# Decoder trunk: each MLP's first weight quarters requested during the projection before it, and attention scores from split queries and keys in a new order

## Time and profile before

| | us |
|---|---|
| median of 3 runs | 1056.5 (1055.74 to 1056.93) |
| the profiled execution's own time | 1058.89 |
| its span | 1057.1 |
| PE busy | 1035.2 (98%) |
| DVE busy | 813.7 (77%) |
| ACT busy | 644.7 (61%) |
| granted clock, mean | 0.994 |

### The profile page before, as it was taken

One profiled execution on the slowest core, in us unless ns is written; L12 is line 12 of the kernel. 1 busy time (PEld: TensorE's weight loads), 2 busy tenths in 40 slices (PEclk: granted clock), 3 DMA queues, 4 the chain that ended last, 5 costly groups with the idle time before them and its releaser, 6 DMA issues.

```text
span 1057.1 us, 15296 instructions
## 1 busy us (share of the span) xinstructions
PE 1035.2 (98%) x5920; PEld 885.5 (84%) x5920; DVE 813.7 (77%) x1157; ACT 644.7 (61%) x940; POOL 108.2 (10%) x133
## 2 busy tenths in 40 slices
PE   8999999999999999999999999999899999999995
PEld 6777889979989989988877777779888988988984
DVE  6988875886896896898656666566598698698697
ACT  7698864745745745665336656566664664664665
POOL 1000021121111101100000000012011011011012
PEclk9999999999999999999999999999999999999998
DMA  7222288498498498462321111167779678779672
GB/s 253 91 81 80 81 229 211 117 252 231 115 256 228 118 258 230 115 173 88 112 63 58 60 60 41 60 187 145 207 143 246 209 151 244 203 152 252 193 156 104
DMA packets 47592, 165.29 MB, mean 156 GB/s; under 512 B 5408, under 2 KB 5536, under 8 KB 47392
## 3 DMA queue, kind: packets, MB, share of 16 engines
q1 hardware_dynamic: 31536, 109.59, 30.2%
q0 software_dynamic: 15552, 53.48, 27.7%
q10 hardware_dynamic: 432, 1.24, 0.3%
HBM read 159.05 MB, written 2.10 MB: 152 GB/s over the span
## 4 chain that ended last, share of the span: by engine, by line
PE 87%; DVE 5%; DMA 5%; ACT 1%; issue 1%; SPq 0%; DVEq 0%; ACTq 0%
PE ps L1982 27%; PE ps L2017 27%; PE ps L1849 21%; DMA w_raw<-weights 5%; PE ps L2080 4%; PE ps L2139 2%; PE ps L2165 2%; DVE w_lo L1120 1%; PE ps L1908 1%; PE ps L2154 1%; DVE value L1499 1%; ACT w_hi L618 1%; DVE acc L1149 0%; DVE q L1452 0%; DVE x_lo L1401 0%
## 5 line engine op out<-in xcount | busy, mean ns | idle before, releaser
L1982 PE MATMUL ps<-x_hi,w_hi 128*128 128x256 f32 x896 | 255.2, 285 | 3.3 <-DVE cols L1170 2.0
L1982 PE MATMUL ps<-x_lo,w_hi 128*128 128x256 f32 x896 | 254.4, 284 | 0.0
L1982 PE MATMUL ps<-x_hi,w_lo 128*128 128x256 f32 x896 | 254.3, 284 | 0.0
L618 ACT ACTIVATE w_hi<-w_raw 128x1024 fp32r<-128x1024 f32 x134 | 140.5, 1055 | 170.2 <-DMA w_raw<-weights 127.8
L1120 DVE TENSOR_TENSOR w_lo<-w_raw,w_hi 128x1024 fp32r<-128x1024 f32 x134 | 163.9, 1224 | 89.4 <-ACT w_hi L618 88.9
L1120 DVE TENSOR_TENSOR w_lo<-q,w_hi 128x1024 fp32r<-128x1024 f32 x144 | 176.3, 1227 | 42.9 <-ACT w_hi L618 42.0
L618 ACT ACTIVATE w_hi<-q 128x1024 fp32r<-128x1024 f32 x144 | 150.9, 1052 | 93.4 <-PE ps L1982 42.1
L2017 PE MATMUL ps<-w_hi,a_hi 128*128 128x512 f32 x448 | 176.2, 393 | 1.8 <-DVE w_lo L1120 1.2
L1982 PEld LDWEIGHTS ps<-x_hi,w_hi 128*128 128x128 f32 x896 | 172.9, 193 | 4.1 <-DVE cols L1170 2.2
L2017 PE MATMUL ps<-w_hi,a_lo 128*128 128x512 f32 x448 | 174.6, 390 | 0.0
L2017 PE MATMUL ps<-w_lo,a_hi 128*128 128x512 f32 x448 | 174.5, 390 | 0.0
(11 more groups left out here) (218 smaller groups left out, 1666.8 us busy)
## 6 DMA issues: line engine op xcount, KB each, us to landing
w_raw<-weights SPq DMA_DIRECT2D x134, 512.0 KB, 4.4
q<-weights POOLq DMA_DIRECT2D x96, 512.0 KB, 8.1
q<-weights SPq DMA_DIRECT2D x64, 512.0 KB, 4.6
x<-x_t SPq DMA_DIRECT2D x8, 256.0 KB, 6.6
y_t<-value SPq DMA_DIRECT2D x8, 256.0 KB, 2.3
acc<-work POOLq DMA_DIRECT2D x6, 256.0 KB, 3.3
rstd<-work POOLq DMA_DIRECT2D x6, 256.0 KB, 3.5
w_raw<-weights SPq DMA_DIRECT2D x4, 256.0 KB, 4.7
```

The lines of the kernel that those rows point to most:

```text
L618: nc.scalar.activation(w_hi[:, t % RING, :], src, ACT.Copy).then_inc(whi_done, 1)
L1982: ins = nc.tensor.matmul(to, w[:, t % RING, ws], o[:, op, j, :], start=fresh and j == 0 and f % 2 == 0 and n == 0, stop=j == PAIRS - 1 and ...
```

## The change

Two parts.

1. Loads. `q1` and `q2` now lie at the start of their memory region, over `in_hi` (first layer) and `h_hi` (second). SP requests A21 for `q2` and `q1` in the middle of the projection's own loads (`first_quarters`), after waiting for `tile_done` of the products that used that place. POOL's `add_first` now also issues the A11 addition to `q1`, ahead of `accumulate`.
2. Scores. Queries and keys are split: ACT copies each to fp32r (`query_hi`, `key_hi`), DVE subtracts in place (`query_lo`, `key_lo`), and a score is three fp32r matmuls for each map in place of one float32 matmul. The lists of PE, ACT and DVE in the attention are in a new order; `scores(h, 0)` and `scores(h, 1)` are neighbours, for the last head also 2 and 3.

```diff
         region = ExitStack()
+        q1 = sb("q1", [P, 2, TILE], F32, region)
+        q2 = sb("q2", [P, 2, TILE], F32, region)
...
+        kq_lo = sb("kq_lo", [P, 2, 2, S], F32R, early)
+        early.close()
         kq = sb("kq", [P, 2, 2, S], F32)
...
+        kq_hi = (att_hi[:, HEADS - 2:, :], att_lo[:, HEADS - 2:, :])
...
-                    elif layer:
-                        sp.wait_ge(scores_mm, QB * HEADS)
                     else:
-                        sp.wait_ge(olo_done, O_M0)
+                        sp.wait_ge(tile_done, (T_OUT, T_O)[layer])
...
             for r in range(RAWS, R_MLP0):
                 load_ring(r, r)
+                if r == R_MLP0 - RING:
+                    first_quarters(0)
...
+                if r == R_MLP1 - RAWS - 1:
+                    first_quarters(1)
...
             def add_first(layer, g):
                 add_quarter(layer, g, "q2", A22, loaded=0)
+                add_quarter(layer, g, "q1", A11, loaded=0)
...
+            def key_hi(h):
+                act.wait_ge(bank_read, T_QK - SHIFT + 2 * h + 2)
+                nc.scalar.activation(kq_hi[0][:, h % 2, :], kq[:, h % 2, 0, :], ACT.Copy).then_inc(kq_hi_done, 1)
...
+            def key_lo(h):
+                dve.wait_ge(kq_hi_done, 2 * h + 2)
+                nc.vector.tensor_tensor(kq_lo[:, h % 2, 0, :], kq[:, h % 2, 0, :], kq_hi[0][:, h % 2, :],
+                                        ALU.subtract).then_inc(kq_lo_done, 1)
...
-                    pe.wait_ge(bank_read, T_QK - SHIFT + 2 * h + 2)
+                    pe.wait_ge(kq_lo_done, 2 * h + 2)
...
+                for i, (q, k) in enumerate(((q_hi, k_hi), (q_lo, k_hi), (q_hi, k_lo))):
+                    for c in range(2):
+                        rows = slice(c * HEAD_DIM, (c + 1) * HEAD_DIM)
+                        ins = nc.tensor.matmul(ps[:, BANK_SCORES + 2 * (j % 2) + c, 0:n], q[rows, :], k[rows, :],
+                                               start=i == 0, stop=i == 2)
...
             for h in range(HEADS - 1):
                 kq_part(h + 1, 0)
+                kq_part(h + 1, 1)
+                if h > 1:
+                    back(h - 2)
+                kq_part(h + 1, 2)
+                if h:
+                    attend(h - 1, 0)
+                    transposes(h - 1, 2)
+                    attend(h - 1, 1)
                 scores(h, 0)
...
                 scores(h, 1)
...
                 if h:
                     transposes(h - 1, 3)
...
+                kq_part(h + 1, 4)
+                kq_part(h + 1, 5)
+                kq_part(h + 1, 6)
                 transposes(h, 0)
...
+                kq_part(h + 1, 7)
+                scores(h, 2)
                 transposes(h, 1)
...
                 scores(h, 3)
```

More of the change, by code:

```diff
@@ L341, in build @@
         sub_gain_done = sem("sub_gain_done")
+        kq_hi_done = sem("kq_hi_done")
+        kq_lo_done = sem("kq_lo_done")
         scores_mm = sem("scores_mm")
@@ L1010, in _ @@
             act.wait_ge(sub_gain_done, 1)
-            split_hi(T_QK + RING)
-            for h in range(HEADS):
-                last = h == HEADS - 1
+            query_hi(0)
+            key_hi(0)
+            for h in range(HEADS - 2):
+                split_hi(T_QK + 2 * h + RING)
                 if h:
                     transposed(h - 1, 2)
-                split_hi(T_QK + 2 * h + 1 + RING if not last else T_QK + 2 * h + RING)
+                split_hi(T_QK + 2 * h + 1 + RING)
+                if h:
+                    transposed(h - 1, 3)
@@ new lines, in _ @@
+            h = HEADS - 2
+            split_hi(T_QK + 2 * h + RING)
+            transposed(h - 1, 2)
+            split_hi(T_QK + 2 * h + 1 + RING)
+            transposed(h - 1, 3)
+            exps(h, 0)
+            squares(h - 1)
+            exps(h, 1)
+            sub_guess_of(h - 1)
+            transposed(h, 0)
+            split_hi(T_O + 2)
+            scaled(h - 1)
+            transposed(h, 1)
+            query_hi(h + 1)
+            key_hi(h + 1)
+            attended_hi(h - 1)
@@ L1051, in _ @@
+            split_hi(T_O + 3)
+            transposed(h + 1, 2)
+            transposed(h + 1, 3)
+            squares(h + 1)
+            sub_guess_of(h + 1)
+            scaled(h + 1)
+            attended_hi(h + 1)
             residual_step(1, T_O, T_O - SHIFT, N_M1, ("mlp_norm", NCH))
@@ L1745, in _ @@
             key(0)
[L1746 to L1751, removed]
-            for h in range(HEADS - 2):
+            query_lo(0)
+            key_lo(0)
+            for h in range(HEADS - 2):
+                biased(h, 0)
+                biased(h, 1)
+                split_lo(T_QK + 2 * h + RING)
+                combined(h, 0)
+                if h:
+                    variance(h - 1)
@@ L1753, in _ @@
                 query(h + 1)
+                combined(h, 1)
+                if h:
+                    sub_newton(h - 1)
                 split_lo(T_QK + 2 * h + 1 + RING)
+                biased(h, 2)
+                key(h + 1)
+                query_lo(h + 1)
                 biased(h, 3)
                 combined(h, 2)
-                key(h + 1)
                 if h:
                     attended_lo(h - 1)
-                split_lo(T_QK + 2 * h + 2 + RING)
+                key_lo(h + 1)
@@ L1761, in _ @@
+                combined(h, 3)
                 halved(h)
[L1762 to L1769, removed]
-            h = HEADS - 2
[L1771 to L1776, removed]
@@ L1788, in _ @@
             biased(h, 3)
+            query_lo(h + 1)
+            key_lo(h + 1)
+            attended_lo(h - 1)
             combined(h, 2)
-            split_lo(T_QK + 2 * h + 1 + RING)
-            attended_lo(h - 1)
+            halved(h)
             combined(h, 3)
+            biased(h + 1, 0)
+            biased(h + 1, 1)
+            combined(h + 1, 0)
+            split_lo(T_O + 2)
             variance(h)
             sub_newton(h)
+            combined(h + 1, 1)
+            biased(h + 1, 2)
@@ L1795, in _ @@
+            biased(h + 1, 3)
+            combined(h + 1, 2)
             attended_lo(h)
+            combined(h + 1, 3)
+            split_lo(T_O + 3)
+            variance(h + 1)
+            sub_newton(h + 1)
+            attended_lo(h + 1)
             residual_step(1, T_O)
```

125 lines of the change are left out of this document (58 added, 67 removed).

## The result

The changed kernel takes 1042.68 us (median of 4 runs, 1042.32 to 1043.27), against 1056.55 for the kernel before on the same chip (4 runs): ratio 0.987, 95% interval 0.9853 to 0.9887. I had forecast 1041.0 with a range of 1036 to 1047.5; the time lies inside, 1.7 us over the forecast. The profiled execution took 1043.27 us, 15.6 less than the one before. That is the predicted 15.5 to 0.1; between the medians it is 13.9, since the profiled execution before lay 2.3 over its median and this one 0.6. The closeness of 15.6 to 15.5 is partly luck: the three stages that I forecast gained 14.5, two of the three terms are off in opposite directions, and about 1 us comes from start-up work that the change does not touch.

What follows compares the result with a forecast made beforehand. PE, busy 98% of the span, was taken as the bound. Part 1 (loads) 10.2 us plus part 2 (scores) 5.3 made 15.5 off the 1056.5 median: 1041.0 us, range 1036 to 1047.5.

Steps and rivals of the forecast that it cites:

- First MLP, 3.6 predicted: Moved loads and additions end PE's 2.2 us pause before up product 3 and the 1.2 GHz stretch behind it.
- (b): Rival: A12 tile still late in the first MLP or both MLPs, 1044 to 1047 us; chance 0.11 with (e).
- the clock's term: First MLP: the 3.41 us stretch at 1.2 GHz goes with the pause, worth 1.4 us.
- Second MLP, 6.6 predicted: DVE on time 1.5 us, pause before the transposes 3.4, slow stretch about 1.7, all gained from moved loads.
- no longer shares the engines with the quarter loads and additions: Second MLP: ACT's tile comes clear of them, so DVE enters the last residual step on time: 1.5 us.
- the 1.7 us for the slow stretch: Second MLP: stretch holds 13 matmuls where 31 would fit, less 0.7 us of pause already counted: about 1.7 us.
- Attention, 5.3 predicted: Part 2 on PE: 0.66 us for each of six middle heads (4.0), first head 0.3, last 1.0.
- A visit: Attention: entering the score blocks costs 0.30 us; four visits a head become three, in the last head two.
- (a): Rival in the scores: the two maps do not run together in fp32r, part 2 loses about 6, 1052 us; chance 0.07.
- (c): Rival in the attention: key_lo late by a steady 1 us a head, part 2 gives nothing, 1046 to 1047; chance 0.08.
- (d): Rival in the attention: key_lo chain over 3.1 us late a head, change slower, 1063 us at 4 us; chance 0.04.
- (e): Rival in the loads: first_quarters waits so late for tile_done that nothing moves; chance 0.11 together with (b).

Runs made afterwards that it cites:

- e6: Changed kernel with POOL's A11 additions to q1 back behind the squares, loads still early: 1045.15 us, ratio 0.9884.
- e4: Changed kernel with the second MLP's first quarters requested one ring load earlier: 1041.9 us, ratio 0.9849.
- e1: Kernel before with the loads' edits only, float32 scores and old orders kept: 1048.2 us, ratio 0.9911.
- e3: Changed kernel with float32 score products, no splits of queries and keys, new orders and loads kept: 1045.55 us, ratio 0.9884.
- e9: Changed kernel with transposes(h - 1, 3) again between scores(h, 0) and scores(h, 1) in six heads: 1045.64 us, ratio 0.9887.
- e8: Changed kernel with map 1's score matmuls left out: 1041.51 us (one run).
- e5: Changed kernel with each score block's fp32r matmuls reordered, three of map 0 and then three of map 1: 1044.04 us, ratio 0.9869.
- e11: Changed kernel measured again with no edit: 1044.55 us, ratio 0.9885.
- e2: Kernel before with the scores' edits only, loads and additions of the first quarters as before: 1048.55 us, ratio 0.9914.

## Why the prediction was right, and where it was not

**First MLP, 3.6 predicted, 3.8 measured.** Pause and slow stretch gone. I expected the tile in 6 to 7 us, with a limit of 8.5; it took 4.5. Rival (b) says that the load's own length is not in the trace before. It is: the ring load of 696.21 landed in 3.5 us. e6 shows that the additions' place does it. It also shows that the lower clock did not follow from the pause by need: e6 has the pause without a slow stretch and loses 2.3 us, before has both and loses 3.8, so the clock's term, put at 1.4, was 1.5.

**Second MLP, 6.6 predicted, 4.2 measured.** The step that failed reads: the tile for which ACT waited "no longer shares the engines with the quarter loads and additions". The tile of output tile 6 does share them: 8.43 us, ACT waits 5.27. I had looked at the wait of the earlier trace rows and checked that the quarters were gone by then; I did not check which ring load would stand beside the additions at their new place. The price by its parts, against e4: 0.47 at 711.00; 0.3 before the transposes; 1.5 for the lower clock; together 2.3 of the 2.45 us. In e1 this step of the prediction costs nothing (ACT waits 2.5 us and the stage is clean), with 15.2 us between quarters and ring load; part 2's order cut that to 12.4. Part 1 alone was costed right (10.2 predicted, 3.8 and 6.7 in e1), and its meeting with part 2's order on the DMA engines was not costed at all. e4, which only moves the quarters away, gets the 2.45 back. Within the 6.6, the 1.7 us for the slow stretch does not come out of its row: 3.41 × (1 - 13/31) less 0.7 is 1.3. That e1 gave 6.7 in all shows the sum of the three terms, not each of them.

**Attention, 5.3 predicted, 6.5 measured.** Both terms were sized too low. The products give 0.30 us a head (e3), not 0.21: for 128 keys I charged 0.20 us over the columns' time because no fp32r step under 0.12 us was in the trace. The steps are 0.16 and 0.12 us, and with the exit the block takes 0.48 us from its start to the next matmul, against 0.42 for the float32 one in e3, a loss of 0.06; 0.23, 0.18 and 0.12 us are the steps for 512, 384 and 256 keys. A visit costs 0.40 us (e9), not 0.30: I counted both edges of the score blocks but not that the transpose between two visits is slower too. Over eight heads the first gives 0.7 more, and the order's 4.10 against 3.6 gives 0.5: the missing 1.2.

**The overhead of a step.** Pairs of 512 columns start 0.23 us apart, of 256 columns 0.12, where the columns alone are 0.213 and 0.107: some 0.015 us a step of two matmuls, as in the full array. Pairs of 128 columns start 0.11 to 0.12 apart too (598.36, 598.48), where the columns alone are 0.053, and so do the one-column float32 sums (721.26, 721.37). So a step has a floor of some 0.11 us here, and above it costs little more than its columns. The Trainium skill, page "TensorEngine Tiling (Array Packing)", Performance Considerations, Instruction Overhead, gives each matmul some 60 cycles of overhead; by the prediction's estimate from that figure part 2 would have given 3 us. The trace does not agree for the steps of 512 to 256 columns, which have 0.015 us where two times 60 cycles at 2.4 GHz would be 0.05 by estimate; for 128 columns the trace has 0.06.

**The rivals.** (a) is excluded by e8. (b), a late A12 tile, did not come; a late ring load came in its stead. (c) and (d), a late `key_lo`, did not come either: 17.78 of 17.78 us of the head are PE's. (e) fell with the issue times, 110.55 and 672.47.

**What stays open.** When the clock falls after a short pause. e5 has the same orders in the second MLP as the changed kernel, pauses of 0.47 and 0.3 us in the same places, and no slow stretch:

```profile
724.90:728.30 3.40, 3.40 (x31) 3.40 (x30) 2.15 (x2) 3.37 (x7) 0.86 (x1) 1.00 0.99 169
```

That window of e5 covers the place, 0.2 to 1.2 us behind the start of the transposes that follow the sums, where the changed kernel, e9 and e11 have 0.50. e3, with a longer pause (0.70) and the same second one, has none either. In each of these kernels the 16 one-column matmuls of the norm's sums and 8 transposes lie between; nothing I varied tells the cases apart, and the 1.5 us is shown only as what a slow stretch costs where it comes. e2's second MLP is 1.85 us shorter than before without part 1. Its trace has no pause in up product 0, where before lost 1.5: the last tile for which ACT waits long is copied at 704.73, 7.0 us ahead of that MLP, where before had it 1.9 ahead, so DVE has caught up. Its pause before the transposes is 2.6 us where it was 3.4. Which of the new orders does this was not tested.

## What to carry to other kernels

When a load is moved out of one collision, list what else is requested until the last of the additions that hang on it has landed (20 us here, from 672.47 to 692.84), and do that after the other edits' shifts are in. A collision with a load that has room costs nothing (e4). In these kernels additions by accumulating DMA are the neighbours to keep away from a tile that PE will need soon. When an instruction moves on one engine, move what reads it on the next engine's list as well, or the wait only changes its owner.

## What the runs showed of the hardware

- Matmuls on the upper and lower 64 rows start within 0.01 us of each other even where the program queues three for one half before the three for the other (e5): order between the halves cost 0.05 us in 186.5.
- A visit to the 64-row form between 128-row work costs 0.40 us, of which nearly half falls on the 128-row matmuls beside it (e9).
- A tile of 512 KB landed in 3.4 to 3.6 us with no addition in flight or with one about to land (e4's at 684.86, e6's at 687.70) and in 4.5 beside two accumulating DMAs issued after it. It took 8.4 us behind three that were left of four, and 10.5 to 10.7 beside four (before, e2, e6). In the changed kernel the DMA engines were full in the 8.4 us:

```profile
684.87:693.30 8.43, 8.41 (x37) 6.95 (x38) 4.75 (x9) 3.12 (x5) 0.00 (x0) 1.00 0.97 253
```
